# Modulation rows turned into columns by VectorE block transposes, and a fold that streams 8 columns in four column groups

## What is computed

```python
for i in range(DEPTH):                                 # DEPTH = 2
    mod = jax.nn.silu(c) @ w_ada[i] + b_ada[i]         # w_ada[i]: 1024 x 6144
    sh1, sc1, gt1, sh2, sc2, gt2 = jnp.split(mod[:, None, :], 6, axis=-1)
    modc = jax.nn.silu(c_ctx) @ w_ada[i] + b_ada[i]
    sh1c, sc1c, gt1c, sh2c, sc2c, gt2c = jnp.split(modc, 6, axis=-1)
    h = modulate(rmsnorm(x, g_norm1[i]), sh1, sc1)     # h * (1 + scale) + shift
    hc = modulate(rmsnorm(xc, g_norm1[i]), sh1c, sc1c)
    ...
```

## Time and profile before

| | |
|---|---|
| median of 3 runs | 2841.44 us (2841.38 to 2844.13) |
| span of the profiled execution | 2839.6 us |
| TensorE busy | 2597.9 us (91%) |
| its weight loads | 1560.4 us (55%) |
| VectorE busy | 812.8 us (29%) |
| ScalarE busy | 449.4 us (16%) |
| weights read | 661.12 MB |

### The profile page before, as it was taken

One profiled execution on the slowest core, in us unless ns is written; L12 is line 12 of the kernel. 1 busy time (PEld: TensorE's weight loads), 2 busy tenths in 40 slices (PEclk: granted clock), 3 DMA queues, 4 the chain that ended last, 5 costly groups with the idle time before them and its releaser, 6 DMA issues.

```text
span 2839.6 us, 31122 instructions
## 1 busy us (share of the span) xinstructions
PE 2597.9 (91%) x13399; PEld 1560.4 (55%) x13399; DVE 812.8 (29%) x1772; ACT 449.4 (16%) x1009; POOL 60.6 (2%) x91
## 2 busy tenths in 40 slices
PE   8999999999999999999999998987999998666665
PEld 5678888568886444444444442333556786332322
DVE  2535511335602553333112121112344412110101
ACT  1320010131001022121111101113111311100001
POOL 1010000000000100000000000000100000000000
PEclk9999999999999999999999999999999999777777
DMA  8676453474444310221438999999521358999997
GB/s 298 221 192 173 163 163 133 154 235 149 159 162 152 110 60 31 74 74 59 171 118 361 413 421 421 421 421 390 187 88 61 134 228 340 421 421 421 420 421 312
DMA packets 202972, 664.29 MB, mean 234 GB/s; under 512 B 14226, under 2 KB 60596, under 8 KB 153940
## 3 DMA queue, kind: packets, MB, share of 16 engines
q1 hardware_dynamic: 193952, 641.97, 59.1%
q0 software_dynamic: 8688, 20.28, 2.9%
q10 hardware_dynamic: 196, 0.06, 0.0%
HBM read 661.12 MB, written 9.57 MB: 236 GB/s over the span
## 4 chain that ended last, share of the span: by engine, by line
PE 74%; DMA 20%; DVE 3%; ACT 2%; issue 1%; ACTq 0%; DVEq 0%
PE ps L519 40%; DMA ring<-in_w_e 20%; PE ps L1195 8%; PE ps L540 8%; PE ps L743 5%; PE ps L1145 1%; PE ps L1172 1%; PE ps L715 1%; PE ps L635 1%; PE ps L999 1%; PE ps L1021 1%; PE ps L954 1%; PE ps L967 1%; PE ps L942 1%; PE ps L651 1%
## 5 line engine op out<-in xcount | busy, mean ns | idle before, releaser
L519 PE MATMUL ps<-normed,ring 128*128 128x256 f32 (+1 forms) x3392 | 915.8, 430 | 4.7 <-ACT normed L2105 2.5
L519 PEld LDWEIGHTS ps<-normed,ring 128*128 128x128 f32 x3392 | 642.4, 191 | 254.9 <-issue 178.8
L1195 PE MATMUL ps<-ring,arena 128*32 128x256 f32 (+1 forms) x4344 | 589.4, 528 | 179.2 <-DMA ring<-in_w_e 173.6
L1195 PEld LDWEIGHTS ps<-ring,arena 128*32 128x32 f32 (+1 forms) x4344 | 194.3, 133 | 554.2 <-DMA ring<-in_w_e 263.3
L519 PE MATMUL ps<-arena,ring 128*128 128x256 f32 (+1 forms) x832 | 254.0, 462 | 1.3 <-DVE small L1321 1.3
L540 PE MATMUL ps<-ring,normed 128*128 128x512 f32 x512 | 222.8, 593 | 0.0
L519 PEld LDWEIGHTS ps<-arena,ring 128*128 128x128 f32 x832 | 156.1, 190 | 88.1 <-issue 73.1
L1402 DVE COPY arena<-ps 128x256 f32<-128x256 f32 (+1 forms) x102 | 55.7, 554 | 401.3 <-PE ps L519 145.8
L540 PEld LDWEIGHTS ps<-ring,normed 128*128 128x128 f32 x512 | 96.2, 190 | 116.6 <-issue 116.4
L743 PE MATMUL ps<-arena,ring 128*128 128x256 f32 x704 | 152.3, 379 | 0.0
L743 PEld LDWEIGHTS ps<-arena,ring 128*128 128x128 f32 x704 | 133.8, 190 | 18.2
(11 more groups left out here) (266 smaller groups left out, 1847.5 us busy)
## 6 DMA issues: line engine op xcount, KB each, us to landing
ring<-in_w_e SPq DMA_DIRECT2D x363, 1024.0 KB, 20.3
ring<-in_w_in SPq DMA_DIRECT2D x56, 1024.0 KB, 7.4
ring<-in_w_ada SPq DMA_DIRECT2D x48, 1024.0 KB, 7.6
ring<-in_ffn_w_up SPq DMA_DIRECT2D x88, 512.0 KB, 6.4
ring<-in_ffn_w_down SPq DMA_DIRECT2D x22, 1024.0 KB, 5.6
ring<-in_dil_w_qkv SPq DMA_DIRECT2D x18, 1024.0 KB, 5.2
arena<-in_w_e SPq DMA_DIRECT2D x16, 1024.0 KB, 9.1
ring<-in_sb_w_qkv SPq DMA_DIRECT2D x12, 1024.0 KB, 15.0
```

The source lines that it names most:

```text
L519: ins = mm(o[:, 0:n], slots[k // 4][:, k % 4, f * P:(f + 1) * P], src[:, k, 0:n], start=k == 0, stop=k == kts - 1)
L1195: ins = mm(o[w * g:w * g + w, 0:cols], lhs(2 * c + j), part, start=c == 0 and j == 0, stop=c == KT // 2 - 1 and j == 1)
```

## The change

ScalarE's copy of a part is replaced by a transpose on VectorE, 128 x 512 in blocks of 32 x 32 (`ada_turn`), which writes the same `ada_rows`. After it, column 32j + r of a block row holds, on partition m of group a, row r of group a, column 32j + m. The fold then has the constant (its first 32 columns) as weights, and as data two of each 32 columns, 8 columns in all for each of the four column groups; its output is dense, 128 x 8. The bank of a part has VectorE as its reader, so the steps of VectorE's list come in the order part's bank, fold's bank as TensorE opens them: `ada_steps`, `ada_gap`, `ada_pairs` and, in the routers and in the last layer, single calls of `ada_turn` ahead of the columns. All of ScalarE's calls of `ada_copies` go. Nothing moves in TensorE's list or in the stream of weights.

```diff
--- before.py
+++ after.py
@@ -108,7 +108,7 @@
     first = np.clip(col - NA_WIN_C // 2, 0, GRID_W - NA_WIN_C)
     inside = (col[None] >= first[:, None]) & (col[None] < first[:, None] + NA_WIN_C)
     put("col_neg", np.tile(np.where(inside, 0.0, NEG), (2, 1)))
-    put("fold32", (k[:, None] % 32 == k[None, :]) & (k[None, :] < 32))
+    put("fold32", k[:, None] % 32 == k[None, :] % 32)
     return t
 
 
@@ -629,14 +629,14 @@
                 for slot, loaded, count in next_chunks(2):
                     pe.wait_ge(loaded, count)
                     slots.append(slot.rearrange("p (k n) -> p k n", k=4))
-                o = banks.open("a")
+                o = banks.open("v")
                 pe.wait_ge(*banks.due)
                 for k in range(KT):
                     ins = mm(o[32 * (k % 4):32 * (k % 4) + 32, :], silu_pad[:, k, :], slots[k // 4][:, k % 4, :],
                              start=k < 4, stop=k >= 4)
                 ins.then_inc(banks.filled, 1)
                 chunks_done(2)
-                ada["read"][ada["part"]] = sum(r[-1] == "a" for r in banks.uses)
+                ada["read"][ada["part"]] = sum(r[-1] == "v" for r in banks.uses)
                 ada["part"] += 1
 
             def ada_fold():
@@ -644,11 +644,12 @@
                 n = ada["fold"]
                 ada["fold"] += 1
 
-                pe.wait_ge(banks.freed["a"], ada["read"][n])
+                pe.wait_ge(banks.freed["v"], ada["read"][n])
                 o = banks.open("v")
                 pe.wait_ge(*banks.due)
-                for f in range(4):
-                    ins = mm(o[:, f * P:f * P + 32], ada_rows(n)[:, f * P:(f + 1) * P], cst("fold32")[:, 0:32], start=True, stop=True)
+                turned = ada_rows(n).rearrange("p (f q r) -> p q f r", q=4, r=32)
+                for q in range(4):
+                    ins = mm(o[32 * q:32 * q + 32, 0:8], cst("fold32")[:, 0:32], turned[:, q, :, 0:2], start=True, stop=True)
                 ins.then_inc(banks.filled, 1)
 
             def ada_next():
@@ -1430,6 +1431,19 @@
 
             ada_done = [0]
 
+            ada_turned = [0]
+
+            def ada_turn():
+
+                o = banks.take("v")
+                v.wait_ge(banks.filled, banks.at["v"])
+                ve.transpose(ada_rows(ada_turned[0]), o).then_inc(banks.freed["v"], banks.free("v"))
+                ada_turned[0] += 1
+
+            def ada_turn_next():
+                ada_turn()
+                ada_column()
+
             def ada_column():
 
                 i, c = divmod(ada_done[0], N_MOD * D // BRANCH)
@@ -1437,13 +1451,20 @@
                 o = banks.take("v")
                 v.wait_ge(banks.filled, banks.at["v"])
                 bada = b_ada[:, i * N_MOD * KT + 4 * c:i * N_MOD * KT + 4 * c + 4]
-                ve.tensor_tensor(mods[i][:, 4 * c:4 * c + 4, :], o.rearrange("p (f s) -> p f s", s=P)[:, :, 0:2],
+                ve.tensor_tensor(mods[i][:, 4 * c:4 * c + 4, :], o[:, 0:8].rearrange("p (f s) -> p f s", s=2),
                                  bada.unsqueeze(2).broadcast_to([P, 4, 2]), ALU.add
                                  ).then_inc(banks.freed["v"], banks.free("v"))
 
-            def ada_columns(count):
-                for _ in range(count):
-                    ada_column()
+            def ada_steps(count):
+                return [ada_turn] + [ada_turn_next] * (count - 1) + [ada_column]
+
+            def ada_gap(count):
+                for step in ada_steps(count):
+                    step()
+
+            def ada_pairs():
+                for step in (ada_turn, ada_turn, ada_column, ada_column):
+                    step()
 
             def amplitudes(i, which, ns):
 
@@ -1463,7 +1484,7 @@
                                      ).then_inc(xn_ready.sem, xn_ready.up())
 
             def ffn(i):
-                ada_columns(ADA_MIXER)
+                ada_gap(ADA_MIXER)
                 v.wait_ge(rstd_ready.sem, rstd_ready.nth("v"))
                 cw = conv_w[:, i * CONV_W * 2 * FT:(i + 1) * CONV_W * 2 * FT]
                 cb = conv_b[:, i * 2 * FT:(i + 1) * 2 * FT]
@@ -1509,7 +1530,7 @@
                         amplitudes(0, 0, 2)
                         times_rstd(S, 2 * S)
                 mixer_out(SM, gain_of(i, 3))
-                ada_columns(ADA_BLOCK[i])
+                ada_gap(ADA_BLOCK[i])
 
 
             v.wait_ge(rstd_ready.sem, rstd_ready.nth("v"))
@@ -1573,7 +1594,7 @@
             fill = [lambda T=T, t=t: scaled(T[:, t, :]) for T in (SQT, SKT) for t in range(4, 8)]
             fill[-1] = lambda: (scaled(SKT[:, 7, :]), second_half())
             staged(2 * SB_HALF, (0, sb_abs), (1, sb_logs), (2, sb_args), (3, lambda b: evac(SOT[:, b, :], S)),
-                   fill=fill, over=SB_HALF, late=[lambda: None] + [ada_column] * ADA_FIRST)
+                   fill=fill, over=SB_HALF, late=ada_steps(ADA_FIRST))
             v.wait_ge(banks.freed["v"], banks.frees["v"])
             stamp().then_inc(o_ready.sem, o_ready.up())
             mixer_out(SM, gain_of(0, 1))
@@ -1626,7 +1647,7 @@
             values = [lambda g=g, t=t: scaled_rows(DV[:, t, g * BRANCH:(g + 1) * BRANCH], t) for g in range(3) for t in range(ST)]
             values[-1] = lambda: (scaled_rows(DV[:, ST - 1, 2 * BRANCH:3 * BRANCH], ST - 1), second_half())
             staged(len(items), (0, dil_soft), (1, dil_norm), (2 * LAG, dil_copy),
-                   fill=values, over=2 * LAG, late=[lambda: None] + [ada_column] * ADA_SECOND)
+                   fill=values, over=2 * LAG, late=ada_steps(ADA_SECOND))
             v.wait_ge(banks.freed["v"], banks.frees["v"])
             stamp().then_inc(o_ready.sem, o_ready.up())
             mixer_out(SM, gain_of(1, 1))
@@ -1657,7 +1678,7 @@
                     amplitudes(i, 0, 2)
                 times_rstd(0, 2 * S if last else S)
                 if last:
-                    ada_columns(ADA_LAYER // 2)
+                    ada_pairs()
 
                 v.wait_ge(loads["lam"], 64 * (i + 1))
                 ve.tensor_tensor(LAMV[:, 0, :], LAMV[:, 0, :], LAMV[:, 1, :], ALU.mult).then_inc(v_step.sem, v_step.up())
@@ -1679,11 +1700,15 @@
 
                 for g in range(4):
                     evac(UT[:, g, 0:qtok], qtok)
+                if last:
+                    ada_turn()
+                    ada_turn()
                 for t in range(qtiles):
                     evac(VG[:, t, :], 512)
                 stamp().then_inc(tile_turn.sem, tile_turn.up())
                 if last:
-                    ada_columns(ADA_LAYER // 2)
+                    ada_column()
+                    ada_column()
 
                 ws = banks.take("v")
                 v.wait_ge(banks.filled, banks.at["v"])
@@ -1919,6 +1944,8 @@
                         ins.then_inc(v_step.sem, v_step.up())
                 ins.then_inc(aff_ready.sem, aff_ready.up())
                 nr = ns * N_EXPERTS
+                for _ in range(ADA_ROUTER[i] - 1):
+                    ada_turn()
                 o = banks.take("v")
                 v.wait_ge(banks.filled, banks.at["v"])
                 at, aw, sc, keep = AT[0:nr, 0, :], AW[0:nr, :], AT[0:nr, 1, :], AT[0:nr, 0, :]
@@ -1941,7 +1968,9 @@
                 ve.tensor_tensor(sc, sc, keep, ALU.mult).then_inc(v_step.sem, v_step.up())
                 v.wait_ge(v_step.sem, v_step.made)
                 ve.tensor_scalar(aw, sc, -1.0, None, ALU.add).then_inc(pos_ready.sem, pos_ready.up())
-                ada_columns(ADA_ROUTER[i] - 2)
+                for _ in range(ADA_ROUTER[i] - 2):
+                    ada_column()
+                ada_turn()
                 o = banks.take("v")
                 v.wait_ge(banks.filled, banks.at["v"])
                 ve.tensor_copy(pos[:, :, 0:nr], o[:, 0:64].rearrange("p (j r) -> p j r", j=ST)[:, :, 0:nr]).then_inc(banks.freed["v"], banks.free("v"))
@@ -1966,7 +1995,8 @@
                     ins = ve.tensor_scalar(SEL0[:, j, q], SEL[:, j, q * N_EXPERTS:q * N_EXPERTS + 4, :],
                                            RCOL[:, ST * q + j:ST * q + j + 1], None, ALU.mult)
                 ins.then_inc(P_ready.sem, P_ready.up())
-                ada_columns(2)
+                ada_column()
+                ada_column()
                 for j in range(ST):
                     ins = pick(j, (1, 2, 3))
                 ins.then_inc(v_step.sem, v_step.up())
@@ -2126,18 +2156,6 @@
                 sc.wait_ge(gate_ready.sem, gate_ready.nth("a"))
                 se.activation(x, x if src is None else src, ACT.Tanh, scale=scale).then_inc(gate_exp.sem, gate_exp.up())
 
-            ada_copied = [0]
-
-            def ada_copy():
-                o = banks.take("a")
-                sc.wait_ge(banks.filled, banks.at["a"])
-                se.activation(ada_rows(ada_copied[0]), o, ACT.Copy).then_inc(banks.freed["a"], banks.free("a"))
-                ada_copied[0] += 1
-
-            def ada_copies(count):
-                for _ in range(count):
-                    ada_copy()
-
             def ffn(i):
```

(12 more changed lines are left out.)

## The result

The changed kernel takes 2854.35 us (median of 5 runs, 2851.56 to 2855.43) beside 2842.4 us (2841.38 to 2847.07) for the kernel before on the same chip: ratio 1.0038, 95% interval 1.0026 to 1.0051. It is slower by 12 us. The profiled execution has a span of 2852.4 us, 12.8 more than before. The forecast was 2848.8 us, 2840 to 2857.

What follows compares the result with a forecast made beforehand. TensorE was taken to bound the kernel (74% of the chain), the weight stream 20%. Savings in tails, last layer and second router against losses in gaps and first router summed to +7.4 us: 2848.8 us, range 2840 to 2857 (own range 2843 to 2854).

Steps and rivals of the forecast that it cites:

- the second rival, the slow transpose: VectorE's transpose takes 1.4 us, adding 6 us in gaps and routers, 2854.8 us in all; chance 13%.
- The late start in the gaps: Four gaps: the fold waits for a transpose behind the post-norm add, so tiles start +2.6, +2.3, +2.6 and +2.3 us later.
- The clock in the gaps: Four gaps: TensorE's idle wait brings the granted clock down, 1.7 us lost in each.
- The rival that the clock holds: Four gaps: the granted clock stays at 1.00, removing 6.8 us, so 2842.0 us and no change; chance 15%.
- The dilated tail: Six folds in TensorE's dense queue save 0.8 us each, -4.8 us (bounds 0 and -5.4).
- the fold keeps its price: Tails, last layer and elsewhere: record count, not columns, sets the fold's cost; +8 us, 2857 us; chance 5%.
- The transpose: VectorE's 128x512 block transpose costs what its copy does, 0.69 us (bounds 0.58 and 1.4).
- The stick-breaking tail: ScalarE's copy of 0.58 us leaves the cycle three times, -1.7 us (bound 0 if VectorE becomes late).
- Last layer: Start: earlier scale and shift, but folds wait for two transposes, -0.4 us; next two folds in dense work, -1.4 us.
- Routers: First router +0.2 us; second -1.1 us, its gather starting 1.4 earlier; bounds -2 and +3 for both.
- The rival on the other side: Behind the gaps TensorE catches up and the delay is swallowed, so only savings count: 2832.6 us, faster; chance 9%.
- a shift at the experts' start is passed on whole: Expert stages: they end on their DMA stream, but the first expert's products must free ring slots, so a start shift carries through.

Runs made afterwards that it cites:

- the clock kept up: The changed kernel, with TensorE running idle 128x512 matmuls (7, 7, 7 and 5) while it waits for the transpose in the four gaps: 2843.4 us, ratio 0.9997.
- the doubled folds: The kernel with the four gaps' six panels left old and the other 18 changed, every fold of a turned block done twice: 2833.63 us, ratio 0.9960.
- the gaps as before: The changed kernel, but the six panels in the four gaps keep ScalarE's copy and the wide fold: 2832.91 us, ratio 0.9960 to the kernel before.
- only the gaps changed: The kernel before, with only the six panels in the four gaps changed: 2867.92 us, ratio 1.0084.

## Why the prediction was right, and where it was off

**The sum.** The sign, the mechanism and the place were right: all four gaps lose and the other places gain. The forecast was 5.5 us short of the median; the table shows where. The median lies 0.35 us outside the forecast's own range (2843 to 2854) and nearest to the time of the second rival, the slow transpose (2854.8). That nearness is chance, since this rival's mechanism fell (below).

**The late start in the gaps** (2.6, 2.3, 2.6 and 2.3 predicted): 2.6, 2.4, 2.6 and 2.4 with the clock kept up. The step by order of VectorE's list, down to the transpose's end and the tiles in front of the square sums, held to 0.1 us.

**The clock in the gaps** (1.7 each, 6.8 in all): 2.5, 1.8, 1.9 and 3.5, or 9.8 in all. This is the term that was mis-sized. I took the shorter spell of the earlier trace rows, 3.4 us at half clock, for all, though TensorE was not idle on end there; the second router, whose wait of 4.51 us I had named as the likeness, had the clock low from 2377.0 to 2383.8, 6.8 us. The traces show spells of 6.8 us at 186, 428 and 623 and of 10.2 at 869. Part of each lies over idle time, so not all of it is lost. In the gap with three folds the spell met the third part and the square sums in the open; there the bound (+5.5) was passed by 0.3. The rival that the clock holds fell: 0.52 and 0.50 in the windows above. By the Trainium skill (TensorE: Matmul & The Clock Gate, "HAM oscillation") idle gaps between bursts bring the clock to half rate; the trace agrees, and its sentence in the prediction, +12.6 for the three gaps, compares with 13.9 measured.

**The dilated tail** (-4.8): -5.6. The fold holds the queue for 0.16 us where I took 0.2, so a fold saves 0.85. It also comes sooner: it starts 1.74 us behind its part's first matmul, where the wide one took 1.86 (573.94 to 575.80 in the kernel before), a step that I had left out. Together five of the folds save 0.97 each and the last 0.77. The rival that the fold keeps its price fell with the rows at 582.55 and with the doubled folds (0.07 us for eight records more).

**The transpose** (0.69): 0.71, so the rival of 1.4 fell. By the Trainium skill (Vector Engine (DVE) Microarchitecture Reference, section 3.8) its front-end is pipelined to one element per cycle and lane, and the trace agrees in that VectorE's copy of the same 128x512 takes 0.69.

**The stick-breaking tail** (-1.7): -1.4 behind a start 0.1 earlier. It agrees, but the size is loose: kernels with the same code there gained 0.3 to 1.5 us in it (0.3 with the clock kept up in the gaps, which had a low stretch of 6.8 us at 140), and the two profiles of the kernel before differ by 1.1 at the same place, as a low stretch at about 138 us is long, short or absent.

**Last layer** (-0.4 and -1.4): -1.2 and -1.3. I gave back too much of the gain to the wait for the transposes and to the clock; the tiles behind the folds are at the lower clock in the kernel before too, for 6.8 us from 1981.0 on, and in the changed one for only 3.4 from 1998.6 on.

**Routers** (+0.2 and -1.1): +0.9 and -1.3. In the first one the gather began 0.6 us earlier, but its low stretch lasted 10.2 us from 1510 on (6.8 in the kernel before) and took 1.5 back. The code is not the cause: with the same router and the gaps as before the stage gained 0.5, and the old router in the kernel with only the gaps changed lost 1.3, with a low stretch of 13.7 us. So my term was about right, and what was missing is the clock.

**Swallowed gains.** The rival on the other side, that the delay is swallowed behind the gaps, fell: the delay of 3.6 us behind the first gap stands unchanged at 400 us, and 12.6 behind the fourth at 1000. The step that a shift at the experts' start is passed on whole held as well: 13.4 us at the first expert of the second block, 13.4 at 2820, though that stage ends on its weight stream.

**What I had no term for**: +2.2 us at 1032 and +1.9 us at the scatter at 1962, both falls of the clock where TensorE works in pieces or waits. Neither is an effect of the changed code at its place: the first is in the kernel before as well, as its second profile shows, the second in the kernel that has the old code there (+1.6) and not in the one with the gaps as before (+0.3). The profile that I built on lacks both, and its execution (2839.6 + 1.8 = 2841.4) was 1 to 2 us better than the medians of the kernel before in the later runs (2842.4 to 2843.6). What decides whether such a stretch comes in a given execution stays open; shifting the whole schedule by some microseconds seems to be enough, but no run tested that by itself.

## What to carry to other kernels

When a step moves to another engine, look first at what stands behind it in the order of the engine that waits: a fold of 0.2 us at the head of a queue, waiting for a transpose of 0.7 us at the tail of another, cost 4 to 6 us a time, while the same fold four tiles later cost 0.4. A cheaper form of an operation is worth having only where nobody waits longer for its input. And where TensorE would stand idle as long as here (4.5 to 6.2 us), price the clock as well as the wait, and try to fill the wait, with useful tiles if there are any, with matmuls of no use if not.

## What I had not expected of the hardware

- Matmuls of no use paid twice: 11 us with them in the gaps of the changed kernel (2854.35 to 2843.4), 4.4 us in the routers of the kernel before.
- The full clock doesn't come back as soon as the work does. In the gap after the first mixer it read 0.50 for 4 us of dense tiles, and in the gap with three folds, where the work behind the wait comes in short pieces, the low stretch was 10.2 us long instead of 6.8.
- In stages in which TensorE works in pieces the same program shows a spell in one profile and none in the next (2.65 us at about 1022), and a last scatter can cost 3 us more or less. One profile of each kernel can't settle a difference of 3 us by its span; a comparison stage by stage shows at least where such a stretch lies.
- Eight float32 records of 128x8 in four column groups added 0.07 us where eight such records already stood, held the queue for 0.16 behind a part, and cost 0.37 between tiles of 128x128. Eight of 128x32 on the whole array held it for 1.0.
